# Transposes of four split-precision stages over four PSUM banks, their products begun at half of the features, and the relative-bias table computed at the start

## What is computed

```python
def second_block(x, mem, ...):
    h = rms_norm_2(x, norm_mix_g[l])
    x = x + hybrid_mixer(h, w_in[l], ..., rel_bias)      # gated convolution and sparse attention
    h = rms_norm_2(x, norm_x_g[l])
    x = x + cross_attention(h, mem, xq_w[l], xkv_w[l], xo_w[l])
    h = rms_norm_2(x, norm_ffn_g[l])
    x = x + swiglu(h, ffn_in_w[l], ffn_out_w[l])
    return rms_norm_2(x, final_norm_g)
```

## Time and profile before

| | us |
|---|---|
| median of 3 runs | 2229.52 |
| lowest and highest | 2221.68, 2230.03 |
| the profiled execution's own time | 2224.64 |
| its span, first to last instruction | 2222.8 |

### The profile page before, as it was taken

The page is one execution under the profiler, slowest core; times in us unless marked ns, Lnnn a source line. Parts: engine busy times, 40 slices in busy tenths (PEclk is TensorE's granted clock), DMA queues, the critical chain, the costliest instruction groups (busy, mean ns, idle before and its releaser), DMA issues.

```text
span 2222.8 us, 21399 instructions
## 1 busy us (share of the span) xinstructions
PE 1923.5 (87%) x8524; PEld 1245.9 (56%) x8524; DVE 667.3 (30%) x1392; ACT 584.6 (26%) x1042; POOL 622.7 (28%) x361
## 2 busy tenths in 40 slices
PE   4999978587878877839999999888888889999997
PEld 2544337432222222218888868544677567888886
DVE  6451355510000000042898024465121211000001
ACT  3113552010000000032232243566243423222212
POOL 0002213300000000023442234555254323555542
PEclk9998999598999999959997998999998998999999
DMA  8354102589999999852222322000233111323231
GB/s 361 151 222 172 46 0 79 208 328 428 427 428 429 428 428 428 367 186 78 98 92 76 95 76 89 26 20 20 95 114 108 44 62 62 114 76 114 76 114 57
DMA packets 96387, 379.14 MB, mean 171 GB/s; under 512 B 8443, under 2 KB 37499, under 8 KB 81964
## 3 DMA queue, kind: packets, MB, share of 16 engines
q1 hardware_dynamic: 90252, 356.58, 41.3%
q0 software_dynamic: 3456, 12.58, 1.5%
q10 hardware_dynamic: 2592, 8.78, 1.0%
HBM read 357.41 MB, written 20.51 MB: 170 GB/s over the span
## 4 chain that ended last, share of the span: by engine, by line
PE 68%; DMA 17%; DVE 7%; ACT 4%; issue 2%; POOL 2%; SPq 0%; DVEq 0%; ACTq 0%; POOLq 0%
DMA slots<-in_w_expert_up 16%; PE bank L702 14%; PE bank L703 14%; PE bank L704 14%; PE bank L677 11%; PE bank L960 6%; PE bank L1165 2%; PE bank L1145 1%; PE bank L745 1%; PE bank L800 1%; ACT area L1653 1%; POOL low_r L2371 1%; DMA slots<-in_w_ada 1%; PE bank L1134 1%; PE bank L1077 1%
## 5 line engine op out<-in xcount | busy, mean ns | idle before, releaser
L2371 POOL TENSOR_TENSOR low_r<-slots,high_r 128x2048 fp32r<-128x2048 f32 x87 | 399.8, 4597 | 630.4 <-ACT high_r L1337 630.4
L703 PE MATMUL bank<-xl_r,high_r 128*128 128x512 f32 (+1 forms) x864 | 332.6, 385 | 0.0
L960 PE MATMUL bank<-slots,area 128*64 128x512 f32 x1024 | 261.7, 670 | 76.7 <-DMA slots<-in_w_expert_gate 41.2
L702 PE MATMUL bank<-area_r,high_r 128*128 128x512 f32 x800 | 315.8, 395 | 4.7 <-DVE xl_r L1788 4.7
L704 PE MATMUL bank<-area_r,low_r 128*128 128x512 f32 x800 | 313.6, 392 | 0.0
L1337 ACT ACTIVATE high_r<-slots 128x2048 fp32r<-128x2048 f32 x87 | 166.2, 1912 | 442.8 <-PE bank L704 418.4
L960 PEld LDWEIGHTS bank<-slots,area 128*64 128x64 f32 x1024 | 79.4, 154 | 258.4 <-issue 162.9
L703 PEld LDWEIGHTS bank<-xl_r,high_r 128*128 128x128 f32 x864 | 165.0, 191 | 31.8 <-issue 0.5
L702 PEld LDWEIGHTS bank<-area_r,high_r 128*128 128x128 f32 x800 | 152.0, 190 | 38.3 <-DVE xl_r L1788 5.9
L704 PEld LDWEIGHTS bank<-area_r,low_r 128*128 128x128 f32 x800 | 151.6, 189 | 31.9
L2198 DVE SCALAR_TENSOR_TENSOR bank<-area,cols,bank 128x512 f32<-128x512 f32 x232 | 153.5, 756 | 0.0
(11 more groups left out here) (367 smaller groups left out, 2713.0 us busy)
## 6 DMA issues: line engine op xcount, KB each, us to landing
slots<-in_w_expert_gate SPq DMA_DIRECT2D x32, 2048.0 KB, 17.9
slots<-in_w_expert_up SPq DMA_DIRECT2D x32, 2048.0 KB, 19.7
slots<-in_w_expert_down SPq DMA_DIRECT2D x32, 2048.0 KB, 20.9
slots<-in_w_in SPq DMA_DIRECT2D x15, 2048.0 KB, 7.9
slots<-in_w_ada SPq DMA_DIRECT2D x11, 2048.0 KB, 12.3
slots<-in_ffn_in_w SPq DMA_DIRECT2D x22, 1024.0 KB, 7.0
slots<-in_ffn_out_w SPq DMA_DIRECT2D x5, 2048.0 KB, 7.9
slots<-in_w_out SPq DMA_DIRECT2D x4, 2048.0 KB, 8.3
```

The source lines that it names most:

```text
L702: nc.tensor.matmul(out, xh, yh, start=start and n == 0, stop=False)
L703: nc.tensor.matmul(out, xh, yl, start=False, stop=False)
L960: last = nc.tensor.matmul(banks[which][piece, :], XT[b][:, k, piece], w[side][:, k, :], start=k == 0, stop=k == KT - 1)
L2371: nc.gpsimd.tensor_tensor(low_half(m), raw_half(m), high_half(m), ALU.subtract).then_inc(s["w_low"], 1)
```

## The change

1. Mix, mem, normx and ffn rotate their transposes over banks 4 to 7, each with a semaphore of its own (`tiles_emptied0` to `3`). Tile n waits for tile n-4. ACT and DVE read from the same rotation.
2. In mix, normx and ffn the products begin right behind the transposes. The wait for the last four tiles stands ahead of the second half of the features of the first product (`later_columns`; for ffin inside its first group of 24, which is now issued as two times 12). In mem the wait stays ahead of the products.
3. The relative bias moves to the start. ACT issues the one-hot and table loads as its third and fourth transfers, POOL sets the last table row first of all, ACT scales the table before it waits for X, PE makes the three products before its first column sums, ACT copies them between the square root and the wait for the reciprocal, and ACT issues the store. The groups "toep" become the first of the program, so that the banks of the first block's groups shift by three. OH, RB, BROW and `lamin` move to other columns of the same tensor, and ACT waits for the store before it writes over BROW.
4. One ACT instruction, a square root of one column, is put ahead of the norm behind the experts. The bias instructions leave the stretch between that norm and the mix stage, and three issues leave SP's queue.

```diff
+plan("toep", ["act"] * 3)
 plan("modcols", ["dve"] * 4, 4)
...
-            sp.dma_start(OH[0:33, :], io["onehot"]).then_inc(s["onehot_loaded"], 16)
-            sp.dma_start(RB[0:32, :], io["rel_bias_2"]).then_inc(s["onehot_loaded"], 16)
...
-            sp.wait_ge(s["act_emptied"], emptied("act", FIRST["toep"] + 2))
-            sp.dma_start(g_dram, BROW[0:NH, :]).then_inc(s["bias_stored"], 16)
...
+            def split_transposes(n, pieces):
+
+                before_it = n - XP["mix"] - N_TILE_BANKS
+                if before_it >= 0:
+                    pe.wait_ge(tiles_emptied[split_bank(n)], before_it // N_TILE_BANKS + 1)
+                for c0, src in pieces:
+                    last = nc.tensor.transpose(banks[4 + split_bank(n)][:, c0:c0 + P], src, ID)
+                last.then_inc(s["xpose_full"], 1)
...
+            def split_emptied(stage):
+
+                for n in range(XP[stage] + KT - N_TILE_BANKS, XP[stage] + KT):
+                    pe.wait_ge(tiles_emptied[split_bank(n)], (n - XP["mix"]) // N_TILE_BANKS + 1)
...
-            norm_transposes("mix", XN4)
+            split_norm_transposes("mix", XN4)
             for n in range(2):
-                split_feature_major(f"glu_g{n}", hTS)
+                split_feature_major(f"glu_g{n}", hTS, later_columns=None if n else "mix")
...
-                    split_product(bank_of(FIRST["ffin"] + 4 * j + n)[:, :],
-                                  [(wh[:, k, c], wl[:, k, c], hTS[0][:, k, :], hTS[1][:, k, :]) for k in range(KT)]
-                                  ).then_inc(s["proj_done"], 1)
+                    bank = bank_of(FIRST["ffin"] + 4 * j + n)
+                    for half in range(2):
+                        if j == n == 0 and half:
+                            split_emptied("ffn")
+                        last = split_product(bank[:, :], [(wh[:, k, c], wl[:, k, c], hTS[0][:, k, :], hTS[1][:, k, :])
+                                                          for k in range(4 * half, 4 * half + 4)],
+                                             start=half == 0, stop=half == 1)
+                    last.then_inc(s["proj_done"], 1)
...
             act.dma_start(k1[:], io["k1"]).then_inc(s["cols_loaded"], 16)
+            act.dma_start(OH[0:33, :], io["onehot"]).then_inc(s["onehot_loaded"], 16)
+            act.dma_start(RB[0:32, :], io["rel_bias_2"]).then_inc(s["onehot_loaded"], 16)
...
+            act.wait_ge(s["onehot_loaded"], 32)
+            act.wait_ge(s["pads_set"], 1)
+            nc.scalar.activation(RB[0:32, :], RB[0:32, :], ACT.Copy, scale=8.0).then_inc(s["bias_rows_ready"], 1)
             act.wait_ge(s["x_loaded"], 16)
             norm(XN1)
+            for n in range(3):
+                width = C if n < 2 else NG - 2 * C
+                bank = full(FIRST["toep"] + n)
+                empty(nc.scalar.activation(BROW[0:NH, n * C:n * C + width], bank[0:NH, 0:width], ACT.Copy))
+            act.wait_ge(s["act_emptied"], emptied("act", FIRST["toep"] + 2))
+            act.dma_start(g_dram, BROW[0:NH, :]).then_inc(s["bias_stored"], 16)
             act.wait_ge(s["norm1_ready"], 1)
...
+            nc.scalar.activation(small[:, 153:154], small[:, 152:153], ACT.Sqrt)
             norm(XN3, s["x_moe"], 1)
```

More of the change, by code:

```diff
@@ L170 @@
 XP = {}
+N_TILE_BANKS = 4
 at = 0
@@ L419, in build, with split_bank @@
         xpose_emptied = [s["bank6_emptied"], s["bank7_emptied"]]
+        tiles_emptied = [s[f"tiles_emptied{i}"] for i in range(N_TILE_BANKS)]
+        def split_bank(n):
+            return (n - XP["mix"]) % N_TILE_BANKS
         emptied_sem = {"act": s["act_emptied"], "dve": s["dve_emptied"]}
@@ L1197, in _ @@
             for c in range(KT):
-                transposes(XP["mem"] + c, [(t * P, MTOK[:, t, c * P:(c + 1) * P]) for t in range(2)])
-            transposed_emptied(XP["mem"] + KT)
+                split_transposes(XP["mem"] + c, [(t * P, MTOK[:, t, c * P:(c + 1) * P]) for t in range(2)])
+            split_emptied("mem")
             for n in range(2):
@@ L1664, in _ @@
             for c in range(KT):
[L1665 removed]
+                nc.scalar.activation(MTS[0][:, c, :], split_transposed(XP["mem"] + c)[:, 0:MEM], ACT.Copy
                                      ).then_inc(s["x_high"], 1)
```

77 lines of the change are left out of this document (37 added, 40 removed).

## The result

| kernel | median (range) | ratio to before, 95% interval | profiled execution, its span |
|---|---|---|---|
| before | 2226.76 us (2221.68 to 2230.03) | | 2224.64, 2222.8 |
| after | 2196.95 us (2190.37 to 2198.72) | 0.9857 (0.9836 to 0.9878) | 2197.94, 2196.1 |

The change makes the kernel faster: 0.0143 of some 2230 us are 31.9 us, with 27 to 37 by the interval, and 29.8 by the two medians. The forecast was 22.6 us and a time of 2206. The direction was right; the gain was a third larger than the sum, and the median lies just under the low end of the range, 2197. The nearest of the cases is "more than the forecast", which had a chance of 0.04, and what came is more than even its 27 us.

A forecast was written before the change was run, and what follows sets the result against it. PE sets the pace nearly everywhere, expert-weight transfers in one stage. Mix 9.8, mem 1.8, normx 5.3 and ffn 6.2, less 0.5 at the start, make 22.6 us: forecast 2206, range 2197 to 2213.

The forecast's parts named there:

- more than the forecast: Case: 3.6 us in mem, 1.4 more in normx, the start free; about 27 us, so 2202; chance 0.04.
- What bounds the kernel, and the pace of the tiles: PE sets the pace nearly everywhere; on four banks the 32 transposes of mix or ffn take 6.5 us, clock rising.
- The second rival: Clock stays low in mix and ffn until the products warm it; gain 18.7 us, 2210.8; chance 0.28.
- the third: Rival: banks don't pace the tiles; only early products, square root and 0.9 gain; 6.0 us, 2223.5; chance 0.05.
- the fourth: Rival: one-hot load lands late at the start, each microsecond past 14.26 costs one; 2241 or more; chance 0.02.
- Mix: Mix stage gains 9.8 us: 7.8 from four banks and early products, 0.9 from moved bias products, 1.1 from table load.
- were on no path of their own: In mix before the change, ACT's three bias copies (0.59 us for a long one) were said to delay nothing themselves.
- mem: Memory stage: eight tiles unbroken on DVE, first product 1.8 us earlier; 3.6 if a half-clock spell behind goes; 1.8 taken.
- normx: Cross-attention stage: first product 4.8 to 5.6 us earlier, 5.3 taken; clock left as is, up to 1.4 more.
- ffn: Feed-forward stage: 5.0 us from the tiles, up to 1.9 from warm products; 6.2 taken, 4.4 with a low clock.
- The start: At the kernel's start, loads cost nothing and bias copies with the store's issue cost 0.5 us; bounds 0 and 2.
- Which time to start from: Profiled 2224.64 gives 2202.0; the median of the runs, 4.9 above, gives 2206.9; the forecast held mostly with the median.

The follow-up runs named there:

- the first trace: First profiled execution of the changed kernel, 2197.94 us, span 2196.1; the changed kernel was timed and traced twice more, 2198.84 and 2196.73 us.
- the two kernels with one half of the change each: Changed kernel with two banks but early products (ratio 0.9936), and with four banks but products behind all eight tiles (0.9912), both against before.
- the kernel with late products: Changed kernel with four banks, but products in mix, normx and ffn waiting for all eight tiles; ratio 0.9912 to before.
- the filler in the gaps: Bias and root move alone (two banks, late products), plus four unread identity transposes behind every second tile of mix, normx and ffn; 2219.95 us, 0.9950 to before.
- the kernel warmed ahead of mix: Changed kernel plus 32 unread identity transposes while PE waits for the norm ahead of mix; 2196.95 us, 0.9849 to before.

## Why the prediction was right in kind and short in size

**What bounds the kernel, and the pace of the tiles: right.** PE at half clock is the pace, 6.1 us for 32 transposes and the handover (6.5 forecast); the clock rises within them; ACT, DVE and POOL keep up. That 6.5 came near is in part luck: it had the rise 4.0 us behind the first transpose, and it came at 5.5 in the first trace; and it had DVE's 0.71 a tile as the pace at full clock, where PE, up to four tiles ahead of DVE, did the last six transposes 0.11 us apart, 0.43 a tile. The two errors offset each other. The second rival (the clock stays low) is out by the rows at 995.26 and 1821.31, the third by the two kernels with one half of the change each, the fourth by 15.07. The Trainium skill, "TensorE: Matmul & The Clock Gate", A second HAM failure mode: psum-queue depth-cycling, ties a swinging clock to pauses between groups. The traces agree with that on pauses (2.32 us of them took the clock away in the kernel with late products) and show that cycling through banks by itself does no harm: four banks in rotation without a pause brought the clock up.

**Mix: 10.5 to 11.2, forecast 9.8.** The parts in the first trace: 0.94 for PE's products and 1.1 for the table (0.9 and 1.1 forecast), 12.80 - 6.13 = 6.67 up to the first product (6.3) and 1.8 for warm products (1.5 within the 7.8 taken). The sentence that ACT's three copies "were on no path of their own" was wrong in before, where they held the first tile by 1.2 us; since the 12.8 of the sum contain that, the sum was not harmed.

**mem: 3.3 in every trace with four banks there, forecast 1.8.** The step took the lower of its own bounds (1.8 and 3.6). DVE in one piece gives 2.1; the other 1.2 are the half-clock spell at the first products, which the upper bound had named and the value taken left out. This is the term that was furthest off in proportion.

**normx: 6.3 to 7.5, forecast 5.3.** The first product is 5.5 us nearer to ACT's first tile, as it should be. That is 0.2 over the forecast. The step then left the clock as it is, with up to 1.4 more; 0.8 to 2.0 came on top. In before PE is at half clock for 10.3 us of this stage, in the changed kernel for 3.4, 3.4 and 0. **ffn: 6.8 to 7.2, forecast 6.2**: the tiles took 6.1 and not 6.5, and the warm products were rated 0.2 too low or more.

**The start: 0.5 to 1.3 in the changed kernel, about 1.0 over nine traces with early loads, forecast 0.5, for the wrong reason.** The forecast had the loads hidden and the copies exposed by half a microsecond. It is the other way round: X landed 0.81 later, and the copies and the store's issue fit. All fourteen traces agree: ACT's first square stands at 15.05 to 15.19 in the nine with early loads and at 14.21 to 14.33 in the five without. The Trainium skill, "DMA: Bandwidth & Descriptors", Issuing engines are not separate DMA queues, had it right: transfers of all issuing engines interleave on the same engines. The estimate by that rule was 0.4, and the trace shows 0.8. In before the transfers were full already; its busy time by stretch (the columns behind PEclk are the DMA share and GB/s):

```profile
10.00:12.00 2.00, 0.00 (x0) 0.00 (x0) 1.16 (x3) 0.21 (x1) 0.00 (x0) 1.00 1.02 414
12.00:14.00 2.00, 0.00 (x0) 0.00 (x0) 2.00 (x4) 0.00 (x0) 0.00 (x0) 1.00 1.13 461
```

So 0.14 MB more on another queue could only come out of X. In the kernels without early loads DVE's row at 34 stands at -0.2 to +0.4.

**The step that failed** is a size, the term for what the clock gives back. The sum priced it at the first products of mix and ffn, took 1.8 for mem from the lower of two bounds, left "the clock as it is" in normx, and put every stretch outside the four stages at nothing. Against the forecast, in the first trace: mix 0.7, mem 1.5, normx 1.0, ffn 0.6, together 3.8 us more. Of these some 2.5 are clock (0.3, 1.2, 0.8 and 0.2) and 1.3 are tiles that went faster than estimated (0.4, 0.3, 0.2 and 0.4). Outside the stages come 2.1 us between 1740 and 1834, in all three traces: there the time at half clock shrinks from 10.2 us to 3.4. Against it stand 0.7 at the start, where the loads were put at nothing, and in the stretch ahead of normx the first two traces win 0.7 and the third loses 2.4. For the first trace 22.6 + 3.8 - 0.7 + 0.7 + 2.1 = 28.5 us; with the 5.1 that two traces of three have besides it is 33.6. The ratios of the three timings are 30 to 35 us. This leaves out the stretch ahead of mix. That the clock is worth this much is shown by experiment in two places: the filler in the gaps (8 us), and mem on two banks, where the half-clock spell at the first products comes back. For the stretches outside the stages it is read from the traces. In all, before spends 325 us of its span at half clock in both traces, the changed kernel 290, 270 and 308.

**Which time to start from** was well chosen: the profiled execution of before was at the low end, and the median of 14 to 17 runs is 2230 in each of the three sets. Against that the changed kernel reads 2196 to 2199.

**What stays open.** Why the half-clock spell in the compressed attention comes in one execution and not in the next, with the same instructions before it, isn't settled; the traces show only that the clock's rise against the first transpose differed (2.8 against 5.4 us). Over the kernels with four banks and early products in mix, the three traces without the spell and with a rise in mix have it 5.4 to 6.1 us behind the first transpose, the four with the spell 2.8 to 5.0: an order, and no cause shown. That the clock's phase decides it is argued from these traces; no run set the phase on purpose and hit a chosen one (the kernel warmed ahead of mix moved the spells, no more). The lag of 1.8 to 10.4 us between the start and mix in the changed kernel stands beside 1.8 in the second trace of before. It goes with the time at half clock there, 212.8, 192.8 and 215.9 us in the three traces, against 192.9 and 192.1 in before. All lags over 4.1 us are of kernels with early loads, and four of these nine traces have 1.8 to 2.6; whether a part of it belongs to the change isn't settled.

## What to carry to other kernels

Where PE hands tiles to two readers in a row, look at what it does between the bursts: on two banks the stop between them cost its own 0.7 us and also the clock, for the tiles and for what follows. Rotate over as many banks as readers and writers need, and start the products as soon as the first half is there. By the medians each part was worth ten microseconds and more here, and they add. A pause of 2.32 us in front of the products undid a clock that had just risen.

When a change removes pauses of PE, price each remaining spell at half clock behind it as well, at half of its length where PE is the bound, and take that as the upper half of the range and not as a footnote.

An early load on an idle queue isn't free when the transfers are full: it delays the load that is waited for.

## What the runs showed of the hardware

- 48 transposes of 128 columns whose output nobody reads, spread over the gaps of two banks in each of three stages (16 a stage), made a kernel faster by 8 us (ratios 0.9986 and 0.9950). The bursts kept their distance of 2.67 us; what changed is the clock.
- A pause of 2.32 us of PE, 1.1 us behind the rise of the clock, was followed by 3.4 us at half clock; in its neighbour without the pause there were none. A pause of 1.79 us, 2.1 us behind the rise, in the kernel warmed ahead of mix, was followed by none.
- Two executions of the same kernel ran the same course for 1206.9 us to within 0.1 us, and a third took 1214.8, with 13.6 us more at half clock between mix and mem. The difference of 7.9 is more than mem, normx or ffn gained, so a single pair of traces can't price such an edit. The lags of a stage agree to 1.2 us between the three traces.
- 0.14 MB more in flight beside a 2 MB load, at a DMA share of 1.0, delayed that load by 0.8 us.
- The kernel before, timed against itself, read 0.9988, with an interval that excludes 1.
